# The second block of a two-block model as straight code: every weight split, context and latent halves apart, attention projections inside the mLSTM loop

## What is computed

```python
for l in range(DEPTH):                      # l = 0 "even", l = 1 "odd"
    hx = modulate(rms_norm(x, norm_g[l, 0]), sh1, sc1)
    hc = modulate(rms_norm(xc, norm_g[l, 0]), csh1, csc1)
    if l % 2 == 0:   # neighbourhood attention (8 heads) beside a two-way mLSTM (4 heads)
        yx, yc = even_mixer(hx, hc, ...)
    else:            # multi-head latent attention, 16 heads, latent queries only
        yx, yc = odd_mixer(hx, hc, ...)
    x = x + g1 * rms_norm(yx, norm_g[l, 1])
    hx = modulate(rms_norm(x, norm_g[l, 2]), sh2, sc2)
    x = x + g2 * rms_norm(conv_ffn(hx, ...), norm_g[l, 3])
    if ctx_out:      # the same for the context in layer 0
        ...
return x

def conv_ffn(h, w_up, conv_w, conv_b, w_down):   # 1024 -> 2 x 2816 -> 1024
    u = dwconv_centred(h @ w_up, conv_w, conv_b)
    a, g = jnp.split(u, 2, axis=-1)
    return (a * jax.nn.silu(g)) @ w_down
```

## Time and profile before

| | |
|---|---|
| time, median of 3 runs | 2564.13 us (2561.41 to 2565.1) |
| time of the profiled execution | 2563.73 us |
| its span, first to last instruction | 2560.6 us |
| PE busy | 2337.0 us, 91% of the span |
| DVE, ACT busy | 1539.7 us (60%), 984.1 us (38%) |
| mean granted TensorE clock | 0.932 |

### The profile page before, as it was taken

The page is one execution under the profiler, slowest core; times in us unless marked ns, Lnnn a source line. Parts: engine busy times, 40 slices in busy tenths (PEclk is TensorE's granted clock), DMA queues, the critical chain, the costliest instruction groups (busy, mean ns, idle before and its releaser), DMA issues.

```text
span 2560.6 us, 34062 instructions
## 1 busy us (share of the span) xinstructions
PE 2337.0 (91%) x13792; PEld 1978.2 (77%) x13792; DVE 1539.7 (60%) x2291; ACT 984.1 (38%) x1365; POOL 231.0 (9%) x251
## 2 busy tenths in 40 slices
PE   7999999999999999995899779959999986896997
PEld 6999879999999979994787445438886433576996
DVE  6877969778877879784330678265553013455741
ACT  5434335335344345333241344135552002544840
POOL 1102212002101222001001300000000000000000
PEclk9999989999999999997999777979999997998999
DMA  5665425665565425661132000112223210003543
GB/s 226 221 232 191 149 82 231 227 236 197 217 232 195 150 104 223 230 225 56 66 132 102 22 1 1 52 58 90 96 98 114 88 58 33 1 34 115 180 156 106
DMA packets 47134, 334.43 MB, mean 131 GB/s; under 512 B 5852, under 2 KB 6972, under 8 KB 8480
## 3 DMA queue, kind: packets, MB, share of 16 engines
q1 hardware_dynamic: 36464, 265.31, 28.4%
q0 software_dynamic: 10544, 67.34, 7.1%
HBM read 331.58 MB, written 1.05 MB: 130 GB/s over the span
## 4 chain that ended last, share of the span: by engine, by line
PE 83%; DVE 12%; ACT 2%; DMA 2%; issue 1%; DVEq 0%; POOL 0%; ACTq 0%; POOLq 0%
PE PS L407 82%; DVE ACC L1786 2%; PE PS L990 1%; DVE RSTD L1934 1%; DVE WLO L1613 1%; DVE PRE L1941 1%; DVE SQ L2215 1%; ACT WHI L1188 1%; DMA X<-in_ctx 0%; DVE B L2096 0%; DMA SC<-in_c 0%; DMA RAW<-in_up_b 0%; DMA RAW<-in_mix 0%; DVE XLO L2015 0%; DVE B L2189 0%
## 5 line engine op out<-in xcount | busy, mean ns | idle before, releaser
L407 PE MATMUL PS<-XHI,WHI 128*128 128x272 f32 (+2 forms) x2656 | 830.0, 314 | 68.4 <-DVE WLO L2020 31.4
L407 PE MATMUL PS<-XHI,WLO 128*128 128x272 f32 (+2 forms) x2656 | 823.9, 312 | 0.0
L407 PE MATMUL PS<-XLO,WHI 128*128 128x272 f32 (+2 forms) x2656 | 800.1, 310 | 0.0
L407 PEld LDWEIGHTS PS<-XHI,WHI 128*128 128x128 f32 x2656 | 512.0, 193 | 95.8 <-issue 71.4
L407 PEld LDWEIGHTS PS<-XHI,WLO 128*128 128x128 f32 x2656 | 511.5, 193 | 20.5
L407 PEld LDWEIGHTS PS<-XLO,WHI 128*128 128x128 f32 x2656 | 500.9, 192 | 20.4
L1613 DVE TENSOR_TENSOR WLO<-RAW,WHI 128x2048 fp32r<-128x2048 f32 x162 | 380.2, 2349 | 155.8 <-ACT WHI L1188 155.8
L1188 ACT CAST WHI<-RAW 128x2048 fp32r<-128x2048 f32 x162 | 307.8, 1904 | 210.8 <-DMA RAW<-in_mix 69.9
L1629 DVE SCALAR_TENSOR_TENSOR AP<-AW,SC,AP 128x512 f32<-128x512 f32 x336 | 241.7, 771 | 0.0
L2020 DVE TENSOR_TENSOR WLO<-RING,WHI 128x2048 fp32r<-128x2048 f32 x54 | 123.5, 2292 | 196.1 <-ACT WHI L1412 196.1
L407 PE MATMUL PS<-G,RING 128*128 128x512 f32 (+1 forms) x704 | 227.4, 486 | 0.0
(11 more groups left out here) (325 smaller groups left out, 2827.8 us busy)
## 6 DMA issues: line engine op xcount, KB each, us to landing
AW<-in_ada POOLq DMA_DIRECT2D x48, 1024.0 KB, 6.4
RAW<-in_up_a SPq DMA_DIRECT2D x44, 1024.0 KB, 4.8
RAW<-in_up_b SPq DMA_DIRECT2D x44, 1024.0 KB, 4.8
RING<-in_up_c SPq DMA_DIRECT2D x44, 1024.0 KB, 4.8
RAW<-in_mix SPq DMA_DIRECT2D x30, 1024.0 KB, 4.8
RAW<-in_dn_a SPq DMA_DIRECT2D x22, 1024.0 KB, 4.8
RAW<-in_dn_b SPq DMA_DIRECT2D x22, 1024.0 KB, 4.9
RING<-in_dn_c SPq DMA_DIRECT2D x16, 1408.0 KB, 6.0
```

The lines of the kernel that those rows point to most:

```text
L407: return pe.matmul(o, w, x, start=first, stop=last)
```

## The change

The loops of the second block are gone. All its in- and out-projections and both parts of its FFNs use split units in the four slots of the first block, with the same helpers `high` and `rest`; only the small up-projections of the odd layer stay unsplit. Down weights come as 11 units of two 128-row blocks for all 8 outputs, as in the first block, and the hidden layer is split as well (HFH, HFL, XB). Norms of the context (z = 0) and of the latent tokens (z = 1) run apart, with own semaphores, statistics and reciprocals, and PE multiplies one half while the other is normed; the first four units of a stage therefore run in halves of 256 columns. The context is loaded and squared during the last FFN of the first block. The six units with queries, keys and values of the attention are multiplied inside the mLSTM loop, six steps (`na_part`) in each item. The norm of the heads is spread over the attention items, with one reciprocal for all heads. Masks are smaller. The bias is loaded after the mLSTM loop. The output is stored in four parts.

```diff
@@ tensor: even layer
-            rms(0, 0)
-            pe.wait_ge(x_split, 4)
-            for n in range(SPLIT_EVEN):
-                s, u = n % 2, U_EVEN + n // 2
...
-                two_tiles_split(s, 0, XLO2).then_inc(unit_done[s], 1)
+            def even_inputs():
+                pe.wait_ge(tile_taken, 8 * 6)
+                in_stat(0, 0, 4)
+                pe.wait_ge(ada_taken, 16)
+                in_stat(0, 1, 7)
+                pe.wait_ge(ln_centred, 4 * 6)
+                half_pair(EVEN0, 0, 0, 0)
+                pe.wait_ge(norm_std[0], in_at(0))
+                pe.wait_ge(ln_std, 7)
+                half_unit(EVEN0 + 2, 0, 4)
+                pe.wait_ge(norm_std[1], in_at(0))
+                half_unit(EVEN0 + 3, 0, 6)
+                half_pair(EVEN0, 0, 1, 0)
...
@@ tensor: mLSTM loop
-            for n in range(ML_ITEMS):
-                if n + 1 < ML_ITEMS:
-                    ml_score(n + 1)
-                ml_turn(n)
+                for n in range(ML_ITEMS):
+                    if n + 1 < ML_ITEMS:
+                        score(n + 1)
+                    na_part(NA_PARTS * n, NA_PARTS)
+                    turn(n)
...
@@ tensor: products over both halves, w_out and the hand-over
+            def full_tile(n, j, bank, ks=range(CT)):
+                for k in ks:
+                    last = three(two(PS[:, bank, :]), n, j * CT + k, XB[:, :, 0, k, :], XB[:, :, 1, k, :], k == 0,
+                                 k == CT - 1)
+                return last
...
-            for n in range(14, 18):
-                s, u = n % 2, U_EVEN + n // 2
-                begin(s, u, u)
-                two_tiles(s, YM2, L2).then_inc(unit_done[s], 1)
-            rms_sums(1, 0, U_EVEN + PAIRS_EVEN)
-            rms(2, 0)
-            pe.wait_ge(x_split, 8)
+                        last.then_inc(y_done[z], 1)
+                        if z == 1 and u == 0:
+                            post_stat(0, 0, 0)
+                        if z == 1 and u == 2:
+                            in_stat(1, 0, 1)
+            def ffn_both():
+                half_pair(FFN0, 1, 0, 0, lambda: post_stat(0, 1, 7))
+                half_unit(FFN0 + 2, 0, 4)
+                in_stat(1, 1, 7)
+                pe.wait_ge(norm_std[1], in_at(1))
+                half_unit(FFN0 + 3, 0, 6)
+                half_pair(FFN0, 1, 1, 0)
...
+                for f in range(4, FT):
+                    pe.wait_ge(conv_taken, conv_at(0, f - 4))
+                    full_unit(FFN0 + f, 2 * (f % 4))
@@ vector: norm of one half
-                for c in range(4):
-                    v.tensor_tensor(PRE[:, 2 * c:2 * c + 2, c0:L2], X[:, 2 * c:2 * c + 2, c0:L2],
-                                    bc(RSTD[:, c0:L2], 2), ALU.mult).then_inc(rm_scaled, 1)
+                for k in range(CT + 2):
+                    if k < CT:
+                        v.scalar_tensor_tensor(PRE[:, k, HALF[z]], X[:, k, HALF[z]], GIN[:, l, w, k, z:z + 1], rst(z),
+                                               ALU.mult, ALU.mult).then_inc(in_scaled[z], 1)
+                    if k >= 2:
+                        j = k - 2
+                        v.wait_ge(in_high[z], CT * e + j + 1)
+                        v.scalar_tensor_tensor(XB[:, z, 1, j, :], PRE[:, j, HALF[z]], MOD[:, l, 24 * w + j, z:z + 1],
+                                               XB[:, z, 0, j, :].bitcast(F32), ALU.add, ALU.subtract)\
+                            .then_inc(in_low[z], 1)
@@ vector, FFN 0, one unit of the straight code
+                for f in range(FT):
+                    side(4 + f, ffn_vec(0, f))
+                    if f >= 1:
+                        rest(FFN0 + f + 3)
+                    product(0, f)
+                    if 16 <= f < 19:
+                        hidden_low(0, f - 16)
@@ gpsimd: the bias, after the mLSTM loop
+            pool.wait_ge(ml_pv, ML_ITEMS)
+            pool.wait_ge(ml_probs, ML_ITEMS)
...
+            pool.wait_ge(tab_loaded, RT_LOADED)
             for r in range(ROWS):
                 for h in range(NAH):
```

More of the change, by code:

```diff
@@ new lines, in full_unit, with token_steps @@
+            def full_unit(n, bank):
+                split(n)
+                for j in range(2):
+                    last = full_tile(n, j, bank + j)
+                last.then_inc(unit2_done, 1)
+            def token_steps(n, bank, half, steps):
+                for step in steps:
+                    t, k = 2 * half + step // CT, step % CT
+                    o = PS[:, bank + half, 256 * (t % 2):256 * (t % 2) + 256]
+                    c = slice(P * (t % 2), P * (t % 2) + P)
+                    wh, wl = (w[:, slot_of[n], k * 256:(k + 1) * 256] for w in (WHI1, WLO1))
+                    xh, xl = (XB[:, t // 2, z, k, c] for z in range(2))
+                    mm(pe, o, xh, wh, k == 0, False)
+                    mm(pe, o, xh, wl, False, False)
+                    last = mm(pe, o, xl, wh, False, k == CT - 1)
+                return last
@@ L1259, in ffn1 @@
                     high(u0 + step + 2)
+                    if i == 3 and step == FT + 4:
+                        act.wait_ge(ctx_loaded, 16)
+                        act.wait_ge(*released[u0 + FT - 1])
+                        for c in range(4):
+                            act.activation(SQC[:, 2 * c:2 * c + 2, :], X[:, 2 * c:2 * c + 2, 0:CTX], ACT.Square)\
+                                .then_inc(in_sq[0], 1)
                 high(u0 + FFN_STEPS)
@@ new lines, in taps_latent, with even_vec @@
+            def taps_latent(c, n, src, vec):
+                act.wait_ge(*released[n])
+                if c >= 2:
+                    act.wait_ge(conv_free, c - 1)
+                cb, ac = CB[c % 2], AC[c % 2]
+                act.copy(cb[:, :, 1, 1:257], src)
+                for a in range(2):
+                    last = act.activation(ac[:, a, 1, :], src[:, a, :], ACT.Identity, scale=vec(a, 1), bias=vec(a, 3))
+                last.then_inc(conv_taken, 1)
+            def even_vec(j):
+                return lambda a, c: EVW[:, 2 * j + a, c:c + 1]
@@ L1756, in ffn1 @@
                     gate_low(step - 1)
+                    if i == 3 and step == 5:
+                        gains(0)
                     if step in (10, 15, 21):
@@ L2082, in top, with attend @@
+            def attend(items, base, probs, banks, between):
                 def top(n):
```

2108 lines of the change are left out of this document (1207 added, 901 removed).

## The result

| | before | after | forecast |
|---|---|---|---|
| time, median of 4 runs | 2564.61 us (2561.41 to 2566.63) | 2373.07 us (2367.43 to 2378.37) | 2351 (2308 to 2412) |
| time of the profiled execution | 2563.73 us | 2378.37 us | 2350.6 |
| its span | 2560.6 us | 2376.6 us | 2347.5 |

The ratio of after to before is 0.9254 (95% interval 0.923 to 0.9278). The profiled execution of after was its slowest of four, 5.3 us over the median.

The account below looks back on a forecast made before the run. PE's product stream, with holes where it waits for norms, was taken as the bound. Stage gains summed to 213.1 us off the profiled 2563.7, giving 2351 us; range 2308 to 2412, the forecast's own bounds 2325 to 2375.

Parts of the forecast that it names:

- rival A: Projections delay mLSTM loop's transposes (16 us more), attention's context items at half clock (14), hand-overs stall 5 each; 2396 us; chance 0.25.
- Prices of the products: PE matmuls everywhere: fp32r 0.226 us on 512 columns, 0.120 on 256; split product 0.678 instead of 0.855 us.
- FFN 0: Second block's first FFN: 394.6 to 370 us, from matmuls, halves, latent sums and 5 us of waits; bounds 362 to 385.
- The shade of the mLSTM loop: mLSTM loop: six attention units lie in the old waits, PE becomes the bound, clock stays up; loop 110 us.
- w_out and the hand-over: w_out up to FFN 0: context half is normed while PE multiplies latent half; 101.7 to 50 us, bounds 48 to 64.
- Gate columns: Behind the in-projections: 96 gate matmuls of 16 columns at 0.142 us each, 13.6 us together.
- Odd attention: Odd layer's attention: PE is bound at full clock, four splits and the extra high part ride along; 69 to 70.5 us.
- Attention: Head norm and attention: 104 to 92 us; context items 1.5 us of DVE work, bias loading just covered; bounds 80 to 115.
- rival B: Attention starts warm and holds its clock, head norm hides, gates cost less: 12 + 6 + 8 less, 2325 us; chance 0.15.
- w_o and norms: Behind the odd attention: 55.7 to 41 us, 23 of products, then 18 in series without an input split behind it.
- norms and odd projections: Behind FFN 0, through the first odd item: halves normed in series on DVE, a gain of 14; 114.7 to 97.5 us.
- Rival D: FFN 1: DVE's 5.0 us per unit grows over 5.75; 15 more, 2366 us; within the forecast's range, no separate chance.

Follow-up runs that it names:

- the variant with the clock at 1.00: Changed kernel with the 96 gate matmuls placed among the sixth unit's wide products, six behind every three: 2363.69 us, ratio 0.9215 to the kernel before.

## Why the forecast was right, and where it was off

**The sum.** Forecast were 213.1 us off, measured 191.5 by the medians and 184.0 by the spans of the two profiled executions. The range held the time. The likeliest case came by its parts, and by its time only just: its own bounds ended at 2375, the median is 2373.07, the profiled execution 2378.37, and 2373 lies as near to the 2396 of rival A as to 2351. What tells the two apart are the stretches. Of A's 45 us, the 16 of the loop and the 15 of the hand-overs did not come (the loop 1.2 us off, w_out and its hand-over 0.3, w_o and its norms 2.2), and of the 14 of the attention's clock at most 4.

**Prices of the products: right.** Every price read from the loops held in straight code, 0.226 and 0.120 us, and 0.855 where the split was undone. FFN 0, FFN 1 and w_out came within 0.3 us each, which is partly luck: FFN 0 was summed from 365 us of matmuls and 5 of waits, and had 367.5 and 2.3. What a halved matmul costs, 0.0136 us, follows from the two prices and was not measured by itself.

**The shade of the mLSTM loop: right, for both reasons that I gave, and worth more than I had thought.** 111.2 us against 110, PE's wait 6.3 instead of 31 us. The products fill the waits, and the loop's own matmuls keep their clock: undoing it cost 39 us, 26 of them in PE's waits for VectorE, the rest in matmuls that take longer (the loop runs at a clock of 0.74 then). Rival A with its thinner shade would have been 126 us here.

**w_out and the hand-over: right.** 50.3 against 50, half a microsecond of wait ahead of FFN 0, and the second block is 20 us longer when the sums stand behind w_out, 14.1 of them in this place.

**Gate columns: the price was mis-sized.** I took 0.142 us each from the earlier trace rows, 13.6 us together. They took 18.2 (1267.3 to 1285.5), and the next unit ran at half clock until 1290.7, which made it 2.1 us longer than in the variant with the clock at 1.00: together 7 us off in a stretch that is off by 5.7. At full clock they cost 0.112 us, less than I had taken; at half clock 0.213. The step that failed is "gate columns 96 x 0.142": it took for granted that a busy PE keeps its clock. The Trainium skill, TensorE: Matmul & The Clock Gate, section LDWEIGHTS (loading the stationary operand), has P/1.2 ns for a weight load, 107 ns for 128 columns; the trace agrees with it at full clock with its 112 ns, and does not at half clock with its 213. By the page the 96 would take an estimated 10.3 us.

**Odd attention: the step that failed most.** "PE is the bound at full clock; four splits and the extra high part ride along." PE was the bound by its busy time, 68.4 of 69.7 us. But an item passes through VectorE, ScalarE, VectorE, PE and ScalarE in turn, and VectorE is busy for 51.8 and ScalarE for 48.8 of those 69.7 us, that is 1.6 and 1.5 us of an item of 2.2. A piece of 1.9 or 2.3 us in that chain is longer than the 0.6 or 0.7 us that an item leaves free. The stage came out 8.5 us longer than forecast, and 9.2 came back without the four splits: 2.3 us for each weight, whose two pieces are 4.2 us long. I had costed it at 1.5 by looking at totals. The extra high part did ride along: without the splits ScalarE is still busy for 9 us more than the 39.6 of before, and the attention takes 69.7 us against 69.0.

**Attention: 4 us off.** The bias was ready at 1469.5 and first used at 1481.3, as forecast, so the cover held. What I left out are the two table loads of ScalarE, 1.28 us each, and the clock: I had priced the context items by VectorE's 1.5 us alone, and from 1453 to 1473 the clock was 0.50. How the 4 us divide between the two was not measured; quarters of the reciprocal changed nothing that can be told. Rival A had these items at half clock throughout, for 14 us; they ran so for a part of them. Of rival B nothing came: its 12 us rested on that clock, and its cheaper gates went the other way.

**w_o and norms: 2.2 off.** The split of FFN 1's first weight, 1.90 and 2.29 us, stood in the chain ahead of the reciprocal, where I had 18 us in series without it. Behind the norm it stood ahead of the other reciprocal instead, and 1.0 us came back.

**The first block: 7.8 us later than before, and no fault of a step.** Its end lies between 1167.5 and 1179.0 in 14 profiles. With the median of the runs instead of the profiled one the forecast is 22 us off, of which 21 lie in the second block (1197.6 measured, 2347.5 - 1171.2 = 1176.3 forecast).

**A sum that does not close.** For the norms and odd projections the row takes 114.7 to 97.5, which is 17.2 us, and the reasons given for it are 14. That 98.0 was measured does not make up for the missing 3.2.

**Rival D did not come:** FFN 1 took 193.7 us with PE busy for 192.8.

## What to carry to other kernels

Here PE's work paid twice when it was put into the waits of a sparse loop: it filled them, and the clock stayed up for the loop's own matmuls. Before you lay a weight split or any other piece of two microseconds into a pipelined loop, compare it with what one item leaves free on that engine, not with the engine's total. In front of and behind the odd attention, in part where the engines wait anyway, the four splits cost nothing that could be seen; inside it they cost 9 to 14 us. When two profiles differ in a part that the change leaves alone, measure from a landmark behind that part: here two profiles of one kernel differed by 3.9 us in their spans and by 0.1 behind that landmark. That 0.1 was luck too, as single stretches that no edit touched differ by up to 3.5 us, so read the stretch that was edited as well.

## What I had not expected of the hardware

- **The clock falls while PE is busy.** With matmuls of 16 columns in a row, PE busy for 2.00 of every 2 us, the granted clock went from 1.00 to 0.50 at 1270 us, after 2.7 us of them, and the same matmuls took 0.213 instead of 0.112 us. With one wide product (three matmuls of 512 columns) to every two gate products (six matmuls of 16) it stayed at 1.00.
- **The same code takes another clock from run to run.** The first block ended between 1167.5 and 1179.0 us, and from 840 to 960 us the granted clock was 0.96 in one profile and 0.93 in another, with its fall before 910 us in the one and behind it in the other.
- **fp32r matmuls of 512 columns take the same time when they are read as two runs of 256**: 0.226 us either way.
